# A fused float32 block on one core: the first two pairs of each feed-forward are formed by eight half products instead of seven, and the hidden rows of the first down pass are read into another buffer

## What is computed

```python
h = h + jnp.square(jax.nn.relu(z @ w_up[l])) @ w_down[l]      # "mlp", hidden width 4096
...
def swiglu(x, w_in, w_out):                                   # "ffn1" and "ffn2", hidden width 2816
    gate, up = jnp.split(x @ w_in, 2, axis=-1)
    return (jax.nn.silu(gate) * up) @ w_out
...
for l in range(DEPTH):
    h = rms_norm_2(x, ffn1_pre_g[l])
    x = x + 0.5 * rms_norm_2(swiglu(h, ffn1_w_in[l], ffn1_w_out[l]), ffn1_post_g[l])
    h = rms_norm_2(x, mix_pre_g[l])
    ...                                                       # attention and a state-space mixer
```

## Time and profile before

| | |
|---|---|
| median of 3 runs | 3139.41 us (3138.13 to 3139.55) |
| profiled execution | 3141.57 us, span 3139.8 us |
| PE busy | 2873.0 us (92%) |
| DVE, ACT, POOL busy | 1717.4, 1183.9, 443.3 us |
| granted clock of PE, mean | 0.961 |

### The profile page before, as it was taken

One profiled execution on the slowest core, in us unless ns is written; L12 is line 12 of the kernel. 1 busy time (PEld: TensorE's weight loads), 2 busy tenths in 40 slices (PEclk: granted clock), 3 DMA queues, 4 the chain that ended last, 5 costly groups with the idle time before them and its releaser, 6 DMA issues.

```text
span 3139.8 us, 35455 instructions
## 1 busy us (share of the span) xinstructions
PE 2873.0 (92%) x13424; PEld 2351.4 (75%) x13424; DVE 1717.4 (55%) x2559; ACT 1183.9 (38%) x1873; POOL 443.3 (14%) x1023
## 2 busy tenths in 40 slices
PE   8998999999999879999505999999999799998999
PEld 7786788788887758888404887897777588887887
DVE  5747666443435687777303355325666866665454
ACT  6524555432323544333102243205663433332332
POOL 0010000100000000789882000002201000000000
PEclk9998999999999989999757999999999899999999
DMA  3121333454441212233115453112213122223544
GB/s 132 41 91 71 121 112 117 181 183 138 154 134 41 101 55 81 96 124 120 40 46 193 145 176 118 47 69 87 92 56 141 61 81 81 81 81 137 169 144 141
DMA packets 100745, 335.76 MB, mean 107 GB/s; under 512 B 12400, under 2 KB 13168, under 8 KB 98272
## 3 DMA queue, kind: packets, MB, share of 16 engines
q1 hardware_dynamic: 82512, 260.08, 24.0%
q0 software_dynamic: 18064, 73.41, 6.4%
HBM read 257.03 MB, written 75.24 MB: 106 GB/s over the span
## 4 chain that ended last, share of the span: by engine, by line
PE 76%; POOL 11%; DVE 5%; DMA 3%; ACT 2%; issue 2%; SPq 0%; DVEq 0%; ACTq 0%; POOLq 0%
PE ps L127 23%; PE ps L129 23%; PE ps L128 23%; POOL tmp_p L1800 2%; POOL tmp_p L1797 2%; POOL tmp_p L1798 1%; DMA hid_raw<-hid 1%; POOL tmp_p L1799 1%; POOL made_osc L1801 1%; PE ps L2251 1%; POOL made_osc L1802 1%; PE ps L2266 1%; PE ps L2225 1%; DMA ssm_mid<-made_out 1%; PE ps L268 1%
## 5 line engine op out<-in xcount | busy, mean ns | idle before, releaser
L127 PE MATMUL ps<-ring_b 128*128 128x512 f32 x832 | 326.2, 392 | 13.9 <-DVE ring_b L1200 13.8
L127 PE MATMUL ps<-mixed_b,up_slots 128*128 128x512 f32 x456 | 181.7, 398 | 158.5 <-ACT late_pieces L895 141.1
L129 PE MATMUL ps<-ring_b 128*128 128x512 f32 x832 | 324.5, 390 | 0.0
L128 PE MATMUL ps<-ring_b 128*128 128x512 f32 x832 | 324.5, 390 | 0.0
L127 PE MATMUL ps<-region_a,up_slots 128*128 128x512 f32 x608 | 241.9, 398 | 36.5 <-DVE up_slots L856 24.3
L849 ACT ACTIVATE up_slots<-weight_sums 128x512 fp32r<-128x512 f32 x240 | 151.6, 632 | 314.7 <-PE ps L129 308.5
L856 DVE TENSOR_TENSOR up_slots<-weight_sums,up_slots 128x512 fp32r<-128x512 f32 x240 | 171.3, 718 | 162.8 <-ACT up_slots L849 162.8
L128 PE MATMUL ps<-region_a,up_slots 128*128 128x512 f32 x608 | 239.7, 394 | 0.0
L129 PE MATMUL ps<-region_a,up_slots 128*128 128x512 f32 x608 | 239.3, 394 | 0.0
L1197 DVE TENSOR_TENSOR ring_b<-hid_raw,ring_b 128x512 fp32r<-128x512 f32 x104 | 72.1, 693 | 292.3 <-ACT ring_b L1190 292.1
L127 PEld LDWEIGHTS ps<-mixed_b,up_slots 128*128 128x128 f32 x456 | 87.5, 192 | 180.0 <-issue 141.9
(11 more groups left out here) (418 smaller groups left out, 6627.8 us busy)
## 6 DMA issues: line engine op xcount, KB each, us to landing
raw<-feed SPq DMA_DIRECT2D x212, 512.0 KB, 3.7
hid_raw<-hid SPq DMA_DIRECT2D x152, 256.0 KB, 3.9
raw<-stream SPq DMA_DIRECT2D x56, 512.0 KB, 3.5
far_raw_b<-feed SPq DMA_DIRECT2D x38, 512.0 KB, 4.4
x_mid<-acc POOLq DMA_DIRECT2D x32, 512.0 KB, 3.1
hid<-late_pieces SPq DMA_DIRECT2D x30, 512.0 KB, 2.6
ssm_row<-ssm_mid POOLq DMA_DIRECT2D x8, 1632.0 KB, 7.6
far_raw_a<-feed SPq DMA_DIRECT2D x22, 512.0 KB, 4.2
```

Source lines behind the costliest of these rows:

```text
L127: nc.tensor.matmul(psum, lhs(0), rhs(0), start=first, stop=False)
L128: nc.tensor.matmul(psum, lhs(0), rhs(1), start=False, stop=False)
L129: return nc.tensor.matmul(psum, lhs(1), rhs(0), start=False, stop=last)
```

## The change

Pairs 0 and 1 of each feed-forward are formed by all eight half products, which makes eight whole products of 24 matmuls (`whole`: th, then p, then u), straight from `one` and `two`, with no weight sums and no joins: ACT applies the curve from PSUM (`whole_act`), and in the gated ones DVE multiplies by the other result (`whole_dve`). The order of rows becomes eight weight splits (each used in both token halves), then (2, 1), (2, 2), and pairs 2 on as before. The second token half is turned, split whole (`far_hi_act`, `far_lo_dve`), and the mixed activations are made under the whole products (`mixed_dve`). Slots become eight, over all of `acc`. Loads of pairs 2 and 3 wait for the splits of rows 0 to 3 and 4 to 7 only. The hidden blocks of the first down pass land in `weight_sums[:, 0]`; only kk = n and n + 1 wait for `hid_free`. The transfers of kk = 2 and 3 are issued before the last store. The parameter work of S5 hangs on earlier rows (38 instead of 52), and POOL no longer waits for a split of pair 1.

```diff
-                order = [(0, 1), (0, 2), (1, 1), (1, 2), (0, 5), (1, 5), (0, 6), (1, 6), (0, 7), (1, 7), (0, 4), (0, 3),
-                         (2, 1), (1, 4), (2, 2), (1, 3)]
+                order = [(p, w) for p in (0, 1) for w in (11, 12, 21, 22)] + [(2, 1), (2, 2)]
...
+                self.whole = [(p, th, u) for th in range(2) for p in range(2) for u in range(2)]
...
+            def row_free(self, i):
+                if i < 8:
+                    return kept[0 if i < 4 else 1], 64 * self.kept_rows
+                if i - SLOTS_UP >= 8:
+                    return self.at("done", i - SLOTS_UP + 1)
+                return self.at("done", self.whole.index(((i - 8) // 4, 1, (i - 8) % 4 // 2)) + 1)
...
+        def whole_act(act, F, j):
+            p, th, u = F.whole[j]
+            if F.gated and u:
+                return
+            dst = F.piece(p, u, th)
+            act.wait_ge(*F.at("done", j + 1))
+            nc.scalar.activation(dst, ps[:, F.bank_at(j), :], ACT.Silu if F.gated else ACT.Relu).then_inc(F.sem["act"], 1)
+            if not F.gated:
+                act.wait_ge(*F.at("act", F.n_act[p, th, u, 0]))
+                nc.scalar.activation(dst, dst, ACT.Square).then_inc(F.sem["act"], 1)
...
         def quick_up_pe(pe, F):
             N = F.norm
+            for j, (p, th, u) in enumerate(F.whole):
+                pe.wait_ge(*F.at("lo", 4 * p + 2 * u + 2))
+                pe.wait_ge(*(F.emptied(j - 4) if j >= 4 else F.banks_free[j]))
+                for k in range(KD):
+                    if p == 0 and u == 0:
+                        pe.wait_ge(*N.at("lo", KD * th + k + 1))
+                    i = 4 * p + 2 * u + k // 4
+                    last = products(ps[:, F.bank_at(j), :], lambda h: up_slots[:, i, h, k % 4 * P:(k % 4 + 1) * P],
+                                    lambda h: F.Z[:, k, h, th * HALF:(th + 1) * HALF], k == 0, k == KD - 1)
+                    if j in (2, 3) and k % 2 == 0:
+                        far_turn_pe(pe, F, 4 * (j - 2) + k // 2)
+                last.then_inc(F.sem["done"], 1)
...
+                    if p == 2 and q in (4, 5, 6, 7):
+                        pe.wait_ge(*F.at("zlo", 4 * {6: 0, 7: 1, 5: 2, 4: 3}[q] + k + 1))
...
+        def hid_place(F, kk):
+            return (weight_sums[:, 0] if kk < F.n else hid_raw)[:, kk % 2, :]
...
             def down(kk):
                 th, k = divmod(kk, F.n)
                 if kk < 2:
                     sp.wait_ge(*F.raw_read(F.pairs - 2))
-                    sp.wait_ge(*F.at("lo", F.place[F.pairs - 1, 1] + 1))
+                    sp.wait_ge(*F.at("lo", F.place[F.pairs - 1, 5] + 1))
+                else:
+                    sp.wait_ge(*F.at("lo", F.N + 2 * kk - 2))
+                if F.n <= kk < F.n + 2:
                     for cond in F.hid_free:
                         sp.wait_ge(*cond)
-                else:
-                    sp.wait_ge(*F.at("lo", F.N + 2 * kk - 2))
...
+            store(F.pairs - 3)
             down(0)
             down(1)
-            store(F.pairs - 3)
             store(F.pairs - 2)
+            down(2)
+            down(3)
             store(F.pairs - 1)
-            for kk in range(2, 2 * F.n):
+            for kk in range(4, 2 * F.n):
...
-            pool.wait_ge(*ffn1.at("lo", ffn1.place[1, 3] + 1))
...
-                     46: lambda: ssm_inverse_dve(dve), 52: lambda: ssm_factors_dve(dve)})
+                     34: lambda: ssm_inverse_dve(dve), 38: lambda: ssm_factors_dve(dve)})
```

More of the change, by code:

```diff
@@ L154, in __init__ @@
                 if not final:
-                    split = 3 * KD // 2 if mixed else 2 * KD
-                    take(self, dict(sq=NT, rms=NT, rinv=NT, xn=NT, tr=2 * KD, hi=split, lo=split))
+                    take(self, dict(sq=NT, rms=NT, rinv=NT, xn=NT, tr=2 * KD, hi=2 * KD, lo=2 * KD))
             def at(self, s, count):
@@ L706, in __init__ @@
                 self.n_join = nth((p, name) for p, q in order for name in self.joins_at(p, q))
[L707 to L711, removed]
+                self.whole = [(p, th, u) for th in range(2) for p in range(2) for u in range(2)]
+                self.n_act = nth([(p, th, u, step) for p, th, u in self.whole if u == 0 or not gated
+                                  for step in range(1 if gated else 2)] +
+                                 [(p, name, step) for p, q in order for name in self.curves_at(p, q)
+                                  for step in range(1 if gated else 2)])
+                self.n_out = nth([(p, th) for p, th, u in self.whole if gated and u] +
+                                 [(p, q) for p, q in order if gated and q in (4, 3)])
+                self.n_sum = {(p, s): 4 * (p - 2) + s for p in range(2, pairs) for s in range(1, 5)}
                 o, other = (OFF_B, "b") if main == "a" else (OFF_A, "a")
@@ L777, in emptied @@
             def emptied(self, i):
+                if i < 8:
+                    p, th, u = self.whole[i]
+                    return self.at("out", self.n_out[p, th]) if self.gated and u else self.at("act", self.n_act[p, th, u, 0])
                 p, q = self.order[i]
@@ L859, in weight_sum @@
         def weight_sum(dve, F, p, s):
-            one, two, S_ = F.raws[2 * (p % 2)], F.raws[2 * (p % 2) + 1], weight_sums[:, 1 if p == 1 else 0]
-            if p >= 2:
-                dve.wait_ge(*F.at("lo", F.place[p - 1 if p > 2 else 0, {1: 5, 2: 6, 3: 7, 4: 3}[s]] + 1))
+            one, two, S_ = F.raws[2 * (p % 2)], F.raws[2 * (p % 2) + 1], weight_sums[:, 0]
+            if p > 2:
+                dve.wait_ge(*F.at("lo", F.place[p - 1, {1: 5, 2: 6, 3: 7, 4: 3}[s]] + 1))
             if s == 1:
@@ new lines, in mixed_hi_act @@
+                dst, src = F.zx[:, 0, dd, 0, :], F.zxf[:, 0, dd, 1, :]
+            elif m == 1:
+                act.wait_ge(*F.at("mixed", 13 + dd))
+                dst, src = F.zx[:, 1, dd, 0, :], F.zxf[:, 1, dd, 1, :]
+            elif m == 2:
+                act.wait_ge(*F.at("done", 8))
+                dst, src = F.Z[:, dd, 0, HALF:], F.zxf[:, 2, dd, 0, :]
+            else:
+                act.wait_ge(*F.at("mixed", 21 + dd))
+                act.wait_ge(*F.at("zlo", 8 + dd + 1))
+                dst, src = F.zx[:, 2, dd, 0, :], F.zxf[:, 2, dd, 1, :]
@@ L1293, in store @@
             def store(p):
+                if p < 2:
+                    for u in range(1 if F.gated else 2):
+                        sp.wait_ge(*(F.at("out", F.n_out[p, 1]) if F.gated else F.at("act", F.n_act[p, 1, u, 1])))
+                        sp.dma_start(hid[p if F.gated else 2 * p + u, :, :], F.piece_pair(p, u).rearrange("p a b -> p (a b)")
+                                     ).then_inc(F.sem[f"stored{p % 2}"], 16)
+                    return
                 if F.gated:
```

309 lines of the change are left out of this document (153 added, 156 removed).

## The result

The changed kernel takes **2944.17 us** (median of 4 runs, 2942.68 to 2944.20), the kernel before 3138.77 (4 runs beside it): ratio 0.9379, 95% interval 0.9363 to 0.9395, 6.2% faster. Forecast: 2938, 2914 to 2966. The profiled execution has a span of 2941.9 against 3139.8 us, so 197.9 us are to be accounted for, where the sum said 201.8.

The account below looks back on a forecast made before the run. POOL's chain was taken to bound the kernel for 141 us. Savings of 69 + 142.8 + 24 less 34 gave 201.8 us, so 2939.8 from the profiled 3141.6, and 2938 as median; range 2914 to 2966.

Parts of the forecast that it names:

- The long wait: PE's 141.1 us wait in ffn1, behind POOL's last S5 store, goes with one restart: 142.8 us saved.
- The starts: Row 0 to row 16 of the three feed-forwards: 23.4 in mlp, 24.9 in ffn1, 20.7 in ffn2, together 69 us saved.
- 53 us and what is left of waits: New start of each feed-forward: whole products 43.5, two more half products 5.4, transposes 4, plus remaining PE waits.
- 6.6 + 1.7: ffn1's product 2: PE waits 6.6 us for splits of rows 4 and 5, plus 1.7 us for a slow-clock restart.
- the 0.7: Wait allowed per feed-forward because DVE's mixed activations fit under products 2 to 7 with nothing to spare: 0.7 us.
- The rival in which DVE and ACT bound the start: Feed-forward starts: PE still waits for DVE and ACT, 10 us in each, POOL shifted too: 2968; chance 0.2.
- The down starts: Starts of the down passes: earlier transfers remove waits at kk = 2 in ffn2, ffn1 and mlp, 24 us saved.
- The new wait: Before ffn1's second down pass (kk = 22): PE waits for POOL's end and restarts, 34 us lost.
- the block beside the down pass: POOL's block beside ffn1's down pass, scaled by DVE's time share (35% against 43%): 49 us, bounds 38.8 and 51.4.
- the prediction's own signs of being wrong: Listed signs: split or `zlo` waits before row 16, POOL blocks beside the down pass at 40 or 52 us, late kk = 0.
- POOL's end comes later: Rival before ffn1's second pass: 51.4 us blocks until DVE idles, or a slower reload; loss 45, 2949; chance 0.1.
- The rival figure of 8 us for the transfers: SP's kk = 22 and 23 transfers, sharing packet by packet with POOL's reload: some 8 us, making the loss 30.

Follow-up runs that it names:

- u1: Changed kernel with hidden rows of the first down pass read into the old buffer again, new order of stores and transfers kept; 3023.04 us, ratio 0.9622.
- p1: Kernel before with only the other buffer for first-pass hidden rows and the new order of stores and transfers on SP; 3031.56 us, ratio 0.9650.
- s1: Changed kernel with four added DVE operations, 10 us in all, at each feed-forward's start; 2968.71 us, ratio 0.9452.
- u3: Changed kernel with the transfers of kk = 2 and 3 of each down pass behind the last store again; 2955.96 us, ratio 0.9407.
- d1: Changed kernel with DVE splitting only 32 of 1024 columns per down weight from kk = 6 in ffn1's first pass; 2931.69 us, ratio 0.9328.
- x1: Changed kernel with POOL's reload of old rows held back until the transfers of kk = 22 and 23 have landed; 2932.15 us, ratio 0.9331.
- a1_unchanged: The changed kernel itself, run again for comparison on the same chip as other follow-ups; 2943.17 us, ratio 0.9372.
- x2_four_more: Changed kernel with hidden rows of kk = 22 to 25 also in the new buffer, ACT waiting before its first normalisation row; 2919.90 us, ratio 0.9294.

## Why the prediction was right

**The long wait** (142.8) went whole: the up pass of ffn1 is 167.8 us shorter where 24.9 + 142.8 = 167.7 stood. That it was the buffer is shown by u1 and p1: without it the wait returns under everything else that was changed, and with it and the order on SP it goes from the kernel before. u1 shows that this order without the buffer does not remove it.

**The starts** (69): 23.2 in mlp, 25.0 in ffn1 when 142.8 is taken as right, and in ffn2 24.9 - 2.3 = 22.6 against 20.7. The bill "53 us and what is left of waits" holds: 62.07 us in ffn1, where 53 + 6.6 + 1.7 + 0.7 = 62.0 was worked out, and 54.49 in mlp (54.3). That both agree within 0.2 is in part luck, since the small terms are off both ways. In mlp the 0.6 lies ahead of row 0, outside the stretch, and instead of the 0.7 there are some 1.5 us of a restart that the sum did not have: behind a wait of 2.0 us ahead of row 0, matmuls at 263 to 266 take 0.63 us where they take 0.39 later. In ffn1 the wait and its restart were longer than 6.6 + 1.7 by about the 0.7 that did not come. In ffn2 the 0.9 at product 1 did not come, and nowhere did the 0.7 for DVE; its layout "with nothing to spare" had about 2.5 us to spare (s1). The rival in which DVE and ACT bound the start is refuted by the trace, but s1 shows how near it was: 9 us more of DVE's work in each feed-forward would have taken 23 us of the 69 back.

**The down starts** (24): 8.9 of 10.3 in ffn2, where waits of 0.96 and 0.24 us are left; 3.9 against 2.5 in mlp with what lies behind it. u3 puts about 9 and 2.3 of this down to the early transfers. In ffn1 the 11.2 can't be read from the change by itself, since the wait for POOL takes up whatever is won ahead of it.

**The new wait** (34): PE wants kk = 22 557.2 us behind row 0 (worked out: 557.0), but resumes at 594.2 instead of 589.8. This is the one term that was visibly mis-sized. Its step that failed is the block beside the down pass, scaled by DVE's share of time, 38.8 + 12.6 x 35/43 = 49 us, and with it the bounds of 38.8 and 51.4. Block 6, of which 40 us lie beside the down pass, took 54.2 where 49.5 was worked out, and block 7 took 51.9; both are longer than the upper bound, and 52 is one of the prediction's own signs of being wrong. Until DVE idles the pace is that of the rival "POOL's end comes later", though not its price of 45. d1 and u1 show the cause as named (DVE's operations with both inputs in SBUF). The scaling failed twice: DVE's share beside block 7 is 20.6 of 51.9 us, 40% and not 35, since its operations take longer there too, and each of its microseconds costs 0.61 us (0.61 in block 6 as well, from 23.8 us of two-input work), where the up pass, from which I scaled, shows 0.50. Why the rates differ is not shown. The landings of POOL's stores add 1.0 and 0.5 us to the two blocks. So POOL's end came at 571 behind row 0 instead of 565, 4.7 of it from block 6 and 2.9 from block 7, with 1 us less ahead of them. Against that, the time from POOL's end to PE's restart was 23.2 instead of 25, the split of kk = 23 ending 20.8 us behind the reload's start where 21 was taken. The rival figure of 8 us for the transfers, which would have made 30 of the 34, did not come: 15.3 us passed, for the reasons under x1.

**What was not foreseen:** 1.4 us in the mixer (last section). With it and the terms above the sum of 201.8 becomes the 197.9 of the spans; the median fell 194.6. The forecast of 2938 also took off 2.2 us because the profiled execution of the kernel before lay that much above its median; that of the changed kernel lies on its median (2944.20 and 2944.17). So of the 6 us between forecast and time 4 come from the sum and 2 from this.

## What to carry to other kernels

When a wait is taken away by giving a reader its own buffer, ask which later reader still shares the old one: here it paid to give the new buffer to four more rows (24 us) and to move the producer earlier (17 us against a1_unchanged), and the second pass no longer waited. When the producer is a slow engine beside a busy one, work out its end from what the busy one does in each stretch, since its pace changes by a third between them. A bulk reload that nobody needs yet should not be issued ahead of the two small transfers on which the bottleneck waits.

## What the runs showed of the hardware

**POOL beside DVE.** A block of about 100 POOL instructions took 38.8 us with DVE idle, 44.9 with 9.2 us of DVE's two-input SBUF work beside it, 51.9 with 20.6. Of these, 1.9, 4.6 and 2.4 us are POOL's wait for a store to land; in block 6 of p1_rows_only it was 5.6, the longest here. DVE paid as well. Groups of DVE's instructions beside block 7 of the changed kernel, mean ns of one:

```profile
L1250 DVE TENSOR_TENSOR ring_b<-raw,ring_b 128x1024 fp32r<-128x1024 f32 x10 | 13.6, 1355 | 1.8 <-ACT ring_b L1241 1.5
L1247 DVE TENSOR_TENSOR ring_b<-weight_sums,ring_b 128x512 fp32r<-128x512 f32 x9 | 7.2, 795 | 28.0 <-ACT ring_b L1240 28.0
```

The same operations take 1.23 and 0.69 us with POOL idle.

**Two queues of transfers.** With both at work, POOL's and SP's moved 564 and 535 packets in 9 us (x1_reload_later's section); SP's first packets moved some 4 us behind its issue.

**A dip of the clock beside a busy PE.** In the mixer of the changed kernel the granted clock falls to 0.98 and 0.97 for two stretches of 32 us, with PE busy as always:

```profile
1935.57:1967.57 32.00, 30.76 (x136) 27.11 (x136) 6.96 (x16) 5.35 (x14) 4.25 (x9) 0.98 0.18 66
1967.57:1999.57 32.00, 31.93 (x275) 24.37 (x273) 20.68 (x55) 21.10 (x43) 6.06 (x12) 0.97 0.24 84
```

It costs 1.4 us. x2_four_more and a1_unchanged have it too (0.98, 0.96); the other ten profiles stand at 1.00 through the same stretches. Both profiled executions of the changed kernel have it, so these runs do not tell whether it goes with the kernel or with the execution. It is the whole of the mixer's unexplained difference, and no edit stands near it; what sets it off stays open.
